# Both mixers' output projections: first half of the columns for all tiles, then the second half from split parts

## The reference

```python
for layer in range(DEPTH):
    ...
    if is_even:
        y_lat, y_ctx = _attn_pool_mixer(...)      # ends with concatenate([a_lat, pool]) @ w_out
    else:
        y_lat = _short_conv_mixer(...)            # ends with (b_gate * z) @ w_out
    ...
    h_lat = _layer_norm(ALPHA * h_lat + m_lat[2] * y_lat, ln_mix_g[layer], ln_mix_b[layer])
    f_lat = _expert_choice_ffn(_modulate(h_lat, m_lat[3], m_lat[4]), w_router[layer], ...)
    h_lat = _layer_norm(ALPHA * h_lat + m_lat[5] * f_lat, ...)
```

## Time and profile before

| | before |
| --- | --- |
| median of 3 runs | 3036.15 us (3035.56 to 3036.36) |
| the profiled execution | 3036.76 us, of which its span is 3034.8 |
| TensorE busy | 2757.2 us (91% of the span) |
| VectorE, ScalarE, GpSimd busy | 1157.1, 792.9, 129.4 us |
| mean granted TensorE clock | 0.961 of full speed |

### The profile page before, as it was taken

How to read it: one execution, slowest core, us unless ns; L and a number is a source line. 1 busy time by engine, 2 the same in 40 slices (tenths; PEclk the granted TensorE clock), 3 DMA queues, 4 the chain that set the end, 5 groups by cost and what they waited for, 6 DMA issues and landing times.

```text
span 3034.8 us, 31945 instructions
## 1 busy us (share of the span) xinstructions
PE 2757.2 (91%) x13380; PEld 1783.2 (59%) x13380; DVE 1157.1 (38%) x1686; ACT 792.9 (26%) x1226; POOL 129.4 (4%) x121
## 2 busy tenths in 40 slices
PE   6987799988889969989888998999999999999998
PEld 4534444433358544433336777878778755487886
DVE  4454511211154351211126654333334588333333
ACT  2343311100032121101014433222232465332222
POOL 1210100000010110000001000000010000000000
PEclk8998899999989979999998999999999999999999
DMA  8960589999923159999992202222241300122320
GB/s 295 319 212 16 206 355 429 427 427 427 428 111 111 43 215 392 428 428 428 425 420 82 84 33 107 83 92 89 84 132 47 81 1 1 56 95 79 111 91 35
DMA packets 125455, 601.03 MB, mean 198 GB/s; under 512 B 7248, under 2 KB 12688, under 8 KB 100480
## 3 DMA queue, kind: packets, MB, share of 16 engines
q1 hardware_dynamic: 120128, 584.27, 48.7%
q0 software_dynamic: 5184, 14.72, 1.6%
HBM read 596.87 MB, written 2.10 MB: 197 GB/s over the span
## 4 chain that ended last, share of the span: by engine, by line
PE 73%; DMA 11%; DVE 11%; ACT 4%; issue 1%; DVEq 0%; POOL 0%; SPq 0%; ACTq 0%; POOLq 0%
PE psum L294 70%; DMA weight_ring<-in_w_exp_down 6%; DVE scratch L244 4%; ACT scratch L282 4%; PE psum L309 3%; DMA scratch<-in_w_exp_down 2%; DMA weight_ring<-in_w_exp_up 2%; DVE scratch L3459 1%; DMA scratch<-in_w_exp_up 1%; DVE scratch L277 1%; DMA weight_ring<-in_w_mix_in 1%; DVE scratch L1396 1%; DVE scratch L257 1%; DVE scratch L1768 0%; DVE scratch L1766 0%
## 5 line engine op out<-in xcount | busy, mean ns | idle before, releaser
L294 PE MATMUL psum<-scratch,scratch 128*128 128x512 f32 (+11 forms) x8984 | 1852.4, 407 | 99.0 <-ACT scratch L282 29.0
L294 PEld LDWEIGHTS psum<-scratch,scratch 128*128 128x128 f32 (+3 forms) x8984 | 1352.2, 183 | 575.2 <-issue 233.4
L294 PE MATMUL psum<-weight_ring,scratch 128*64 128x512 f32 (+2 forms) x2864 | 696.5, 612 | 74.9 <-DMA weight_ring<-in_w_exp_down 26.3
L294 PEld LDWEIGHTS psum<-weight_ring,scratch 128*64 128x64 f32 (+2 forms) x2864 | 232.0, 143 | 492.4 <-issue 399.5
L282 ACT ACTIVATE scratch<-psum 128x512 f32<-128x512 f32 (+4 forms) x330 | 192.9, 585 | 1023.4 <-PE psum L309 557.7
L244 DVE TENSOR_TENSOR scratch<-weight_ring,scratch 128x2048 fp32r<-128x2048 f32 (+2 forms) x110 | 241.9, 2199 | 506.4 <-ACT scratch L282 505.2
L282 ACT ACTIVATE scratch<-weight_ring 128x2048 fp32r<-128x2048 f32 (+2 forms) x114 | 210.2, 1844 | 582.3 <-PE psum L294 559.3
L244 DVE TENSOR_TENSOR scratch<-scratch,psum 128x512 f32<-128x512 f32 x92 | 63.3, 688 | 528.4 <-PE psum L294 526.9
L244 DVE TENSOR_TENSOR scratch<-scratch,scratch 128x512 fp32r<-128x512 f32 (+11 forms) x362 | 215.4, 595 | 64.1 <-ACT scratch L282 51.1
L282 ACT ACTIVATE scratch<-psum,scratch 128x128 f32<-128x128 f32 (+6 forms) x338 | 179.4, 531 | 166.0 <-PE psum L309 67.3
L309 PE MATMUL psum<-consts,scratch 128*128 128x128 f32 (+1 forms) x1020 | 160.5, 298 | 63.0 <-DVE scratch L244 50.8
(11 more groups left out here) (106 smaller groups left out, 691.5 us busy)
## 6 DMA issues: line engine op xcount, KB each, us to landing
weight_ring<-in_w_exp_gate SPq DMA_DIRECT2D x44, 2048.0 KB, 15.8
weight_ring<-in_w_exp_down SPq DMA_DIRECT2D x44, 2048.0 KB, 14.2
weight_ring<-in_w_exp_up SPq DMA_DIRECT2D x43, 2048.0 KB, 15.4
weight_ring<-in_ffn_w SPq DMA_DIRECT2D x28, 2048.0 KB, 7.8
weight_ring<-in_w_mod SPq DMA_DIRECT2D x24, 2048.0 KB, 10.0
scratch<-in_w_exp_up SPq DMA_DIRECT2D x21, 2048.0 KB, 16.1
scratch<-in_w_exp_gate SPq DMA_DIRECT2D x20, 2048.0 KB, 15.8
scratch<-in_w_exp_down SPq DMA_DIRECT2D x20, 2048.0 KB, 13.6
```

The lines of the kernel that those rows point to most:

```text
L294: ins = T.eng.matmul(out, lhsT, rhs, start=start, stop=stop)
```

## The change

Every tile's first half is now made first, as before, four tiles in a row (`whole_tile`). The second half is made afterwards, tile by tile, by `mm3` from split operands (`split_tile`), with `logits_pe` and `turn_pe` between these as before. For this ScalarE rounds the second weight piece in four parts (`weights_hi`) and the four tiles of xT (`input_hi`), and VectorE subtracts to get the low parts, in place (`weights_lo`, `input_lo`). `HalvedNorm` takes the statistics of the first half early (`half_stats`) and keeps them in `first`; the sum is kept in h itself rather than in z.

```diff
+class HalvedNorm(PostNorm):
+    def combine(self, V, t, half):
+        k = self.k
+        job, n = (self.key, "out", t, half), slice(half * HALF, (half + 1) * HALF)
+        zb, hv = self.z_of(t, half), k.h[:, t, n]
+        V.wait_ge(*k.at("full", *job))
+        tt(V, zb, k.psum.of(job), self.row[:, n], ALU.mult, ("free", *job))
+        stt(V, hv, hv, ALPHA, zb, ALU.mult, ALU.add)
+        return hv
+
+    def half_stats(self, V, t):
+        x = self.combine(V, t, 0)
+        V.wait_ge(*V.last())
+        V.eng.bn_stats(self.first[:, t, :], x).then_inc(*V.mark())
+
+    def stats(self, V, t):
+        b = t % 2
+        if t >= self.z.shape[1]:
+            V.wait_ge(*self.k.at(self.key, "h", t - self.z.shape[1]))
+        copy(V, self.st[:, b, 0, :], self.first[:, t, :])
+        x = self.combine(V, t, 1)
+        V.wait_ge(*V.last())
+        V.eng.bn_stats(self.st[:, b, 1, :], x).then_inc(*V.mark())
+        V.wait_ge(*V.last())
+        V.eng.bn_aggr(self.mv[:, b, :], self.st[:, b, :, :]).then_inc(*V.mark())
+        inverse_root_a(V, self.r[:, b, :], self.mv[:, b, 1:2], 1.0, (self.key, "var", t))
+
+    def normal(self, A, t, scale, bias):
+        act(A, self.z_of(t), self.k.h[:, t, :], ACT.Identity, (self.key, "norm", t), scale=scale, bias=bias)
...
+    def weights_hi(self, A, i):
+        k, c = self.k, slice(2 * i, 2 * i + 2)
+        A.wait_ge(*k.at("landed", (self.key, 1)))
+        act(A, self.weights_high[:, c, :], k.ring.pieces[(self.key, 1)][:, c, :], ACT.Copy, (self.key, "weights hi", i))
+
+    def weights_lo(self, V, i):
+        k, c = self.k, slice(2 * i, 2 * i + 2)
+        V.wait_ge(*k.at(self.key, "weights hi", i))
+        tt(V, k.ring.low_pieces[(self.key, 1)][:, c, :], k.ring.pieces[(self.key, 1)][:, c, :],
+           self.weights_high[:, c, :].bitcast(F32), ALU.subtract, (self.key, "weights split", i))
+
+    def input_hi(self, A, t):
+        act(A, self.high[t], self.xT[:, :, t * P:(t + 1) * P], ACT.Copy, (self.key, "x hi", t))
+
+    def input_lo(self, V, t):
+        k, s = self.k, slice(t * P, (t + 1) * P)
+        V.wait_ge(*k.at(self.key, "x hi", t))
+        V.wait_ge(*k.at("full", self.key, "out", t, 0))
+        tt(V, self.low[:, :, s], self.xT[:, :, s], self.high[t].bitcast(F32), ALU.subtract, (self.key, "x split", t))
...
+    def split_tile(self, T, t):
+        k, job = self.k, (self.key, "out", t, 1)
+        low = k.ring.low_pieces[(self.key, 1)]
+        bank = k.psum.take(T, job, (0, 7))
+        T.wait_ge(*k.at(self.key, "x split", t))
+        for c in range(NC):
+            T.wait_ge(*k.at(self.key, "weights split", c // 2))
...
+            mm3(T, bank, (self.high[t][:, c, :], self.low[:, c, t * P:(t + 1) * P]), (self.weights_high[:, c, :], low[:, c, :]),
+                c == 0, c == NC - 1, *names)
...
         for t in range(NT):
-            project_out_tile(self.k, T, self.key, self.xT, t)
+            self.whole_tile(T, t)
+        for t in range(NT):
+            self.split_tile(T, t)
             if t >= 2:
                 self.next.logits_pe(T, t - 2)
             if t:
                 self.next.turn_pe(T, t - 1)
...
         self.norm.spread(A, 0)
+        self.input_hi(A, 0)
+        for i in range(NT):
+            self.weights_hi(A, i)
+        for t in range(1, NT):
+            self.input_hi(A, t)
         for t in range(NT):
...
         self.norm.spread(V, 1)
+        self.weights_lo(V, 0)
         V.wait_ge(*self.k.at("free", self.key, "spread", 0))
+        for t in range(NT):
+            if t:
+                self.weights_lo(V, t)
+            self.norm.half_stats(V, t)
+            self.input_lo(V, t)
         self.norm.norms_dve(V, lambda V: self.next.turned_out(V, NT - 2, 1))
```

More of the change, by code:

```diff
@@ L823, in norm_pool, with __init__ @@
             G.eng.tensor_tensor(k.h[:, t, :], self.z_of(t), self.bias, ALU.add).then_inc(*G.mark((self.key, "h", t)))
+class HalvedNorm(PostNorm):
+    def __init__(self, *args):
+        super().__init__(*args)
+        self.first = self.k.arena(NT, 6)
+    def combine(self, V, t, half):
[23 more added lines that the diff above has]
+        act(A, self.z_of(t), self.k.h[:, t, :], ACT.Identity, (self.key, "norm", t), scale=scale, bias=bias)
 class SumNorm(PostNorm):
@@ L887, in __init__, with places @@
         self.k, self.key, self.before, self.w, self.xT, self.heads = k, key, before, w, xT, heads
-        self.norm = PostNorm(k, key, m["cols"][:, 16:24, 0], gain, bias, layer)
+        self.norm = HalvedNorm(k, key, m["cols"][:, 16:24, 0], gain, bias, layer)
         self.next = None
         self.rest = rest
+    def places(self, x_at, high_at, weights_at):
+        place = self.k.arena.place
+        self.low = place(x_at, (NC, S), F32R)
+        self.high = [place(high_at + t * D, (NC, P), F32R) for t in range(NT)]
+        self.weights_high = place(weights_at, (NC, HALF), F32R)
@@ new lines, in input_hi, with whole_tile @@
+    def input_hi(self, A, t):
[5 more added lines that the diff above has]
+        tt(V, self.low[:, :, s], self.xT[:, :, s], self.high[t].bitcast(F32), ALU.subtract, (self.key, "x split", t))
+    def whole_tile(self, T, t):
+        k, job = self.k, (self.key, "out", t, 0)
+        T.wait_ge(*k.at("landed", (self.key, 0)))
+        w = k.ring.pieces[(self.key, 0)]
+        bank = k.psum.take(T, job, (0, 7))
+        for c in range(NC):
+            names = [("full", *job)] if c == NC - 1 else []
+            if c == NC - 1 and t == NT - 1:
+                names.append(("weights used", (self.key, 0)))
+            mm(T, bank, self.xT[:, c, t * P:(t + 1) * P], w[:, c, :], c == 0, c == NC - 1, *names)
@@ new lines, in split_tile @@
+    def split_tile(self, T, t):
+        k, job = self.k, (self.key, "out", t, 1)
+        low = k.ring.low_pieces[(self.key, 1)]
+        bank = k.psum.take(T, job, (0, 7))
+        T.wait_ge(*k.at(self.key, "x split", t))
+        for c in range(NC):
+            T.wait_ge(*k.at(self.key, "weights split", c // 2))
+            names = [("full", *job)] if c == NC - 1 else []
+            if c == NC - 1 and t == NT - 1:
+                names.append(("weights used", (self.key, 1)))
+            mm3(T, bank, (self.high[t][:, c, :], self.low[:, c, t * P:(t + 1) * P]), (self.weights_high[:, c, :], low[:, c, :]),
+                c == 0, c == NC - 1, *names)
@@ L1568, in __init__ @@
         self.onehot = [place(onehot + g * NT * HALF, (NT, HALF), F32R) for g in range(2)]
+        self.late_at = parts + NT * D, onehot
         self.low = [place(low, (2, D), F32R), place(k.unit_region + SLOT, (2, D), F32R), place(parts + NT * D, (4, D), F32R)]
@@ L3564, in plan @@
         stages[-1].next = experts
+        stages[-1].places(base, *experts.late_at)
         stages.append(experts)
```

## The result

The changed kernel took 3050.43 us (median of four runs, 3049.13 to 3051.57) against 3035.86 for the kernel before: a ratio of 1.0051, with a 95% interval of 1.0039 to 1.0063. It is slower, by some 15 us; the profiled execution took 3049.13. The forecast had the direction and most of the mechanism, but only 8.8 us of it. Against the median the measured time lies at the very end of the range (3050.5), and as a ratio just beyond it (3050.5 / 3036.15 = 1.0047).

A forecast was written before the change was run, and what follows sets the result against it. The mixer stage was taken as bound by TensorE, then by the last tile's norm chain. Mixer losses of 5.0 and 3.8 us made +8.8, giving 3045.0 us against the median of 3036.15; range 3040 to 3050.5.

The forecast's parts named there:

- The products: TensorE, both mixers: a split half takes 5.57 us instead of 6.91, saving 10.7 us in all if TensorE were waited for.
- The splitting at no cost: ScalarE and VectorE make the split parts under TensorE's first halves: cost nothing, with 2 us of cover.
- The norm's chain: Second halves: tiles' norms follow one another every 10.77 us, so tile 3's variance comes 3.3 us later in each mixer.
- The step that failed: VectorE, tile 3's statistics: variance comes 1.71 us after tile 2's h, at 343.7 + 1.71 = 345.4 in the first mixer.
- The lock of the one-column L257: VectorE in tile 3's finish, held by GpSimd on the shared ports: 0.5 us in each mixer, bounds 0 and 0.5.
- The logits in the tail: Tile 2's logits, ahead of tile 3's transpositions, take 3.43 us after a longer TensorE idle time: 1.2 at stake, first mixer.
- The sum: Both mixers: 3.3 + 1.7 = 5.0 us in the first and 3.3 + 0.5 = 3.8 in the second, +8.8 us.
- The shift counted in full: After each mixer: any delay of tile 3's transpositions moves the experts' start and the transfers by as much.
- B: Second halves: the norms overlap and TensorE stays the bound, 4.9 us earlier in each mixer, 3026 us; chance 0.06.
- C: Second halves: TensorE's clock falls in the waits, +3 to +9 us in each mixer, 3050 to 3060 us; chance 0.12.
- D: Both mixers: only the chain's term, without lock and with full clock in the tail, 6.6 or 5.4 us; chance 0.14.
- E: First split product: TensorE waits for the weights' last part, up to 3 us in each mixer, 3051 us; chance 0.04.

The follow-up runs named there:

- the norms first: Changed kernel with each tile's root and norm ahead of the previous tile's copy and evictions on ScalarE: 3036.58 us, ratio 1.0001 to the kernel before.
- the old order: Kernel before, each tile's two halves together, with only the second halves made from split parts: 3023.28 us, ratio 0.9953 to the kernel before.

## Why the prediction was right in its direction and short in its size

- **The products**: right. Whole halves 27.63 us; VectorE read the first split half 33.22 us after the first whole product (312.39 - 279.17), where 27.63 + 5.57 + 0.05 was reckoned.
- **The splitting at no cost**: right. TensorE goes from the whole to the split products without a wait; VectorE's last weight part was there at 304.70, 2.1 us before them.
- **The norm's chain**: right. Tile 0's took 320.62 - 312.39 = 8.23 us, the period is 10.82 and 10.79 (h at 320.62, 331.44, 342.23) against 10.77. The experiment with the norms first shows the cause (7.3 us from tile 0's h to tile 1's), the one with whole products that TensorE's share in it is the first half alone.
- **The step that failed** is "From there bn_stats, the aggregation and L252 take 1.16 more, so the variance of tile 3 is there at 343.7 + 1.71". It takes the operations of before and leaves out the copy at the head of the new `stats`. For tiles 2 and 3 that copy runs into GpSimd's write of h, and pushes the L257 behind GpSimd's next operation: 4.20 us instead of 1.71 for tile 3, 2.5 us in each mixer. With it tile 3's variance came 34.0 us behind the first read of a second half, where the forecast wrote 31.5. Three experiments (no copy, an earlier copy, a reduction) each take it away, and a multiplication in its place brings it back.
- **The lock of the one-column L257** (0.5 us): right as a mechanism, 0.61 against 0.16 without the copy; in the changed kernel it is absent, hidden by the larger delay. Over-counted by 0.5 in each mixer.
- **The logits in the tail**: the start of tile 3's transpositions was put 9.34 us after the variance in the first mixer; it was 8.57, of which 0.5 is the lock and 0.3 a pause of ScalarE in the kernel before that did not come back. In the second it was 8.56 against 9.06.
- **The sum**: 5.0 and 3.8 us were forecast, 6.8 and 6.3 came. The copy gives 2.5 in each, the lock and the tail take back 0.8 and 0.5, and the second mixer's first products took 28.08 instead of 27.63. Without the copy the distances are 3.7 and 4.95 above before, 8.65 in all, against 8.8 on record; that this is so close is luck. The first mixer came out 1.3 below its forecast, since the logits of tile 2 ran partly at the full clock and ScalarE's pause was absent, and the second 1.15 above, since its first products took 28.75 instead of 27.63.
- **The shift counted in full**: right up to the experts. Their first product follows tile 3's transpositions after 38.14 us (393.14 - 355.00), before after 38.12. Behind it not all of it lasts, see below.
- **Rivals**: B did not come, TensorE had its three waits. C came in its harmless form: behind the first wait TensorE's transpositions took 1.98 us and the granted clock up to 328.40 was 0.82, but the h of tile 1 was still waited for at the end of tile 2's work. That wait was 1.18 us, where more than 2 were expected. (C's own sum, +3 to +9 in each mixer on top of 3045, gives 3051 to 3063 and not 3050 to 3060.) D and E did not come.

Left open: a part of the difference between times and distances. The kernels without the copy, or with it out of GpSimd's way, lose 8.5 to 8.8 us in the mixers, and their ratios (1.0014 and 1.0016) say 4 to 5, with intervals that reach to 7.6 and 7.9. The other experiments lean the same way: the old order gains 8.3 us in the mixers, and its ratio says 14. Only the first measurement of the changed kernel says more than its mixers, 14.6 us by the medians against 13.1. The traces show where it lies. Without the copy it took 669.02 us from tile 3's transpositions to the second mixer, of which 631.01 behind the experts' first product, and 1940.2 from the second mixer's transpositions to the end; before it was 671.82, 633.70 and 1943.3. In the first profile of the changed kernel it was 670.67, 632.53 and 1945.35. The programs are the same in these stretches, and TensorE waits for transfers of weights in the first (in all 12.9 and 12.7 us before). What shortens them was not tested.

## What to carry to other kernels

Work that was made cheaper pays only where its engine is waited for: the same split products gained 0.5% in the old order, and in the new one no more than the 1.5 and 0.9 us of the first second half, since moving half of every tile's products to the front left four norms in a row at the end. When a stage is re-ordered, list every instruction of the new sequence, the ones of 0.2 us too, and look for each at what GpSimd does at that moment. A short VectorE copy or multiplication between SBUF places can cost a whole GpSimd operation; keep it out by writing to the final place at once or by using a form that is not held (here a reduction). Issuing it before the wait rather than after also did it, but by a margin of 0.04 us. Where the engine waits for something else anyway, as with the norms first, such a delay costs nothing.

## What the runs showed of the hardware that was not expected

- A copy of 6 numbers per partition took 2.34 us beside a GpSimd addition of 2.34 us that had started 0.02 us earlier, and 0.17 us where it started 0.11 us ahead of one. A multiplication by a constant behaved as the copy (2.34), a reduction did not (0.16).
- A semaphore wait that had long been met, ahead of that copy, was enough to lose that race in both mixers: with it the copy started 0.10 us behind the operation before it, without it 0.03.
